# One stage with one weight ring for merge, output projection and feed-forward, and the second norm's token factor moved behind the products

## The chip, the cores and the metric

The kernel runs on one core of one Trainium2 chip. The metric is the device time of one execution in microseconds (us); a kernel is given as the median of several executions.

## The reference, cut to what matters

One decoder layer for 1,024 prompt tokens and 8 sample tokens, 1,032 in all. The attention and the recurrence ahead of this part are not touched. Their outputs `o_nsa` and `o_hg` enter here:

```python
ga, gb = jnp.split(mg, 2, axis=-1)              # mg: columns of xn @ w_in
y_a = o_nsa @ w_nsa_out
y_b = o_hg @ w_hg_out
x = x + (sigmoid(ga) * y_a + sigmoid(gb) * y_b) @ w_o
xn2 = rms_norm(x, norm2_g)                      # x * rsqrt(mean(x^2) + eps) * g
ext = concatenate([conv_state, xn2 @ w_gate])
c = conv_b + sum(conv_w[j] * ext[:, j:j + L] for j in range(3))
x = x + (silu(c) * (xn2 @ w_up)) @ w_down
```

Outputs of this part are `y`, the last gate rows (`conv_*`) and the window rows (`win_*`), the latter mostly a copy of the old ones. D_MODEL is 1024, D_FF is 2816.

## The kernel before, in words

Channels lie on the 128 partitions and the 1,032 tokens along the free axis, as 8 channel tiles (KD) and three token pieces of 344 (TC).
Every large product is made in three passes (`three_pass`, L305): weights and activations are split into a high part (a rounded copy, ScalarE) and a low part (the rest, a VectorE subtraction), and TensorE accumulates high x high, high x low, low x high. A weight unit is 128 output columns over all 8 channel tiles (512 KB): SyncE loads it into `raw`, ScalarE writes `wh`, VectorE writes `wl` and frees `raw`; two units are in flight. One unit is 3 x 8 x 3 = 72 matmuls of 344 columns.

The last part of the program is this row of blocks:

- `merge_gates` (L321) loops 4 times over two channel tiles. One unit is a pair of gate columns (a and b, two DMAs); for each token piece TensorE makes 48 matmuls for the two gates and then 8 plain fp32 ones for the outputs of the two mixers (L438; each shows as two records). ScalarE takes the sigmoid (L378), VectorE multiplies twice (L409) and adds into `x2` (L413).
- `split_merged` (L444) makes high and low parts of the merged rows in `xh` and `xl`.
- `project_out` (L461) multiplies by `w_o` in 8 units; VectorE adds the product and the residual rows read back from DRAM (L514).
- `norm_to_split` (L242) squares `x2` (L260), adds up (L273), sums over channels with 3 plain fp32 matmuls (L300), takes reciprocal (L279) and root (L262), scales each row by gain and token factor (L290) and splits again (L265, L284).
- `conv_ffn` (L541) has three blocks. The first copies the old window rows DRAM to DRAM (L577, 4 MB) and loads the conv state behind it on the same queue (L580), which TensorE turns (L588) and VectorE copies (L595). The second is the feed-forward: hidden tiles in groups of 6, 6, 6 and 4 (`FF_GROUPS`), per tile a gate unit and an up unit; then 8 down units per group. ScalarE takes the gate product out of PSUM (L633), VectorE does the convolution (L681 to L693), ScalarE Silu (L641), VectorE multiplies with the up product (L698). The third turns the gate tail (L765), copies it (L771) and stores it.
- `store_y` (L784) turns `x2` back (L802), copies it over three buffers and stores it (L830).

Of the kernel before, what the change touches and what calls it, by code (L numbers as in the profile page):

```python
# [10 lines left out]
F32 = mybir.dt.float32  # L11
# [230 lines left out]
def norm_to_split(c, gain, tag):  # L242

    nc = c.nc
    low0 = c.base
    sq = c.low("sq" + tag, [P, 2, NT])
    acc = c.low("acc" + tag, [P, NT])
    rs = c.low("rs" + tag, [P, NT])
    tmp = c.low("ntmp" + tag, [P, 2, NT])
    sqd, added, ssum = c.sem("sqd" + tag), c.sem("added" + tag), c.sem("ssum" + tag)  # L250
    inv, rsq, scaled, hi_done, lo_done = (c.sem(x + tag) for x in ("inv", "rsq", "scaled", "hi", "lo"))
    with nc.Block() as block:

        @block.scalar
        def _(act):
            act.activation(acc[:, :], c.x2[:, 0, :], ACT.Square).then_inc(sqd, 1)
            for k in range(1, KD):
                if k >= 3:
                    act.wait_ge(added, k - 2)
                act.activation(sq[:, k % 2, :], c.x2[:, k, :], ACT.Square).then_inc(sqd, 1)  # L260
            act.wait_ge(inv, 4)
            act.activation(rs[:, :], acc[:, :], ACT.Sqrt).then_inc(rsq, 1)  # L262
            for k in range(KD):
                act.wait_ge(scaled, k + 1)
                act.activation(c.xh[:, k, :], tmp[:, k % 2, :], ACT.Copy).then_inc(hi_done, 1)  # L265

        @block.vector
        def _(dve):
            for k in range(1, KD):
                dve.wait_ge(sqd, k + 1)  # L270
                if k > 1:
                    dve.wait_ge(added, k - 1)
                dve.tensor_tensor(acc[:, :], acc[:, :], sq[:, k % 2, :], ALU.add).then_inc(added, 1)  # L273
            dve.wait_ge(ssum, 1)
            for t in range(3):
                dve.tensor_scalar(rs[:, t * TC:(t + 1) * TC], c.psum[:, t, 0:TC], 1.0 / D, EPS,
                                  ALU.mult, ALU.add).then_inc(inv, 1)
            dve.wait_ge(inv, 3)
            dve.reciprocal(acc[:, :], rs[:, :]).then_inc(inv, 1)  # L279
            dve.wait_ge(rsq, 1)  # L280

            def low_part(k):
                dve.wait_ge(hi_done, k + 1)
                dve.tensor_tensor(c.xl[:, k, :], tmp[:, k % 2, :], c.xh[:, k, :].bitcast(F32),  # L284
                                  ALU.subtract).then_inc(lo_done, 1)

            for k in range(KD):
                if k >= 2:
                    dve.wait_ge(lo_done, k - 1)
                dve.scalar_tensor_tensor(out=tmp[:, k % 2, :], in0=c.x2[:, k, :], scalar=c.ct[:, gain + k:gain + k + 1],  # L290
                                         in1=rs[:, :], op0=ALU.mult, op1=ALU.mult).then_inc(scaled, 1)
                if k >= 1:
                    low_part(k - 1)
            low_part(KD - 1)

        @block.tensor
        def _(pe):
            pe.wait_ge(added, KD - 1)
            for t in range(3):
                mm = pe.matmul(c.psum[:, t, 0:TC], c.ones[:, :], acc[:, t * TC:(t + 1) * TC], start=True, stop=True)  # L300
            mm.then_inc(ssum, 1)
    c.base = low0

def three_pass(pe, out, parts, first=True, last=True):  # L305

# [8 lines left out]
def wait_turn(c, sp, sem, value):  # L315

    sp.wait_ge(sem, value)
    sp.sem_inc(c.turns, 1)

def merge_gates(c, io):  # L321

    nc = c.nc
    low0 = c.base
# [2353 lines left out]
```

## Time and profile before

| | |
|---|---|
| median of 3 runs | 2265.21 us (2257.08 to 2267.87) |
| the profiled execution | 2267.54 us, its span 2265.6 us |
| TensorE busy | 2015.7 us, 89% of the span |
| VectorE, ScalarE busy | 812.5 us (36%), 592.6 us (26%) |
| mean granted TensorE clock | 0.931 of full |
| first matmul of the merge to the last of the feed-forward | 1000.8 to 2237.6 us |

The page gives busy time per engine, the span in 40 slices, and the costliest groups. The windows view cuts the span into stretches and gives for each what every engine did and the clock TensorE was granted (1.00 is 2.4 GHz, 0.50 is 1.2 GHz). The timeline gives single instructions with the idle time ahead of them and what ended it.

### The profile page before, as it was taken

How to read it: one execution, taken by the hardware profiler on the slowest of the kernel's cores; microseconds unless marked ns; L12 is line 12 of the kernel's file. 1: busy time of each engine (PE TensorE's matmuls, PEld its weight loads, DVE VectorE, ACT ScalarE, POOL GpSimd, SP SyncE). 2: the span in 40 equal slices, each digit the busy share in tenths (PEclk: the TensorE clock that was granted, in tenths of full speed). 3: DMA queues.
4: the chain of work that ended last, by engine and by line, in shares of the span. 5: the costliest groups of instructions: out<-in, count | busy, mean ns of one | idle time of the engine just before them, and what ended most of it. 6: DMA issues, size and time to landing. Idle time of an engine off the chain costs nothing. (4 is left out here: it accounts for less than half of the span.)

```text
span 2265.6 us, 40273 instructions
## 1 busy us (share of the span) xinstructions
PE 2015.7 (89%) x16434; PEld 1763.6 (78%) x16434; DVE 812.5 (36%) x1614; ACT 592.6 (26%) x1174; POOL 155.1 (7%) x214
## 2 busy tenths in 40 slices
PE   4999899999776899879999878079999999999997
PEld 3767755655554898768888778079999999999996
DVE  5223045555312466511211122523323333332333
ACT  5133156555202143310110111222212211221221
POOL 3000001000210223300000000000000000000000
PEclk8899869999897999879999989589999999999999
DMA  8324251000335312131211031121111111111112
GB/s 233 55 69 165 106 136 52 1 1 1 103 121 193 105 32 58 40 75 29 56 33 32 0 102 47 66 67 46 44 58 37 44 49 47 46 40 53 47 37 88
DMA packets 164458, 148.04 MB, mean 65 GB/s; under 512 B 7561, under 2 KB 151898, under 8 KB 163466
## 3 DMA queue, kind: packets, MB, share of 16 engines
q1 hardware_dynamic: 153260, 123.77, 18.0%
q0 software_dynamic: 6208, 17.67, 3.1%
q10 hardware_dynamic: 4864, 4.84, 0.9%
q8 instruction: 89, 1.46, 0.3%
q14 instruction: 37, 0.30, 0.1%
HBM read 120.54 MB, written 29.99 MB: 66 GB/s over the span
## 5 line engine op out<-in xcount | busy, mean ns | idle before, releaser
L309 PE MATMUL psum<-xh,fwh 128*128 128x344 f32 x1056 | 339.0, 321 | 7.6 <-DVE fwl L668 7.6
L310 PE MATMUL psum<-xl,fwh 128*128 128x344 f32 x1056 | 338.4, 320 | 0.0
L311 PE MATMUL psum<-xh,fwl 128*128 128x344 f32 x1056 | 338.3, 320 | 0.0
L309 PEld LDWEIGHTS psum<-xh,fwh 128*128 128x128 f32 x1056 | 199.1, 189 | 7.7 <-issue 7.7
L311 PEld LDWEIGHTS psum<-xh,fwl 128*128 128x128 f32 x1056 | 199.2, 189 | 0.0
L310 PEld LDWEIGHTS psum<-xl,fwh 128*128 128x128 f32 x1056 | 199.0, 188 | 0.0
L311 PE MATMUL psum<-hh,fwl 128*128 128x344 f32 x528 | 169.2, 320 | 0.0
L309 PE MATMUL psum<-hh,fwh 128*128 128x344 f32 x528 | 169.2, 320 | 0.0
L310 PE MATMUL psum<-hl,fwh 128*128 128x344 f32 x528 | 169.1, 320 | 0.0
L309 PE MATMUL psum<-xh,mwh 128*128 128x344 f32 x384 | 130.2, 339 | 15.6 <-DVE mwl L394 15.6
L623 ACT ACTIVATE fwh<-fraw 128x1024 fp32r<-128x1024 f32 x76 | 80.3, 1056 | 200.9 <-PE psum L311 197.2
L309 PE MATMUL psum<-wh_n,xh 128*128 128x512 f32 (+3 forms) x288 | 113.3, 393 | 20.5 <-DVE wl_n L913 20.5
L310 PE MATMUL psum<-xl,mwh 128*128 128x344 f32 x384 | 123.6, 322 | 0.0
L311 PE MATMUL psum<-xh,mwl 128*128 128x344 f32 x384 | 123.5, 322 | 0.0
L309 PE MATMUL psum<-xh,r_wh 128*128 128x344 f32 x288 | 103.5, 360 | 7.8 <-DVE r_wl L1578 7.8
L310 PE MATMUL psum<-wl_n,xh 128*128 128x512 f32 (+3 forms) x288 | 109.2, 379 | 0.0
L311 PE MATMUL psum<-wh_n,xl 128*128 128x512 f32 (+3 forms) x288 | 108.9, 378 | 0.0
L409 DVE TENSOR_TENSOR msg<-msg,psum 128x344 f32<-128x344 f32 x48 | 22.4, 509 | 238.4 <-ACT msg L378 238.4
L309 PEld LDWEIGHTS psum<-hh,fwh 128*128 128x128 f32 x528 | 99.3, 188 | 0.0
L311 PEld LDWEIGHTS psum<-hh,fwl 128*128 128x128 f32 x528 | 99.3, 188 | 0.0
L310 PEld LDWEIGHTS psum<-hl,fwh 128*128 128x128 f32 x528 | 99.2, 188 | 0.0
L713 DVE TENSOR_TENSOR x2b<-x2b,psum 128x1032 f32 (+1 forms) x32 | 39.3, 1230 | 165.0 <-PE psum L311 165.0
(422 smaller groups left out, 3746.1 us busy)
## 6 DMA issues: line engine op xcount, KB each, us to landing
fraw<-in_w_gate SPq DMA_DIRECT2D x22, 512.0 KB, 3.8
fraw<-in_w_up SPq DMA_DIRECT2D x22, 512.0 KB, 3.9
fraw<-in_w_down SPq DMA_DIRECT2D x24, 384.0 KB, 3.1
cmp_pages<-in_cache_kv SPq DMA_DIRECT2D x64, 128.0 KB, 2.1
mraw<-in_w_in SPq DMA_DIRECT2D x16, 512.0 KB, 5.5
raw_n<-in_w_in SPq DMA_DIRECT2D x24, 256.0 KB, 3.5
r_raw<-in_w_in SPq DMA_DIRECT2D x12, 512.0 KB, 3.9
xh_copy<-xh SPq DMA_DIRECT2D x1, 4128.0 KB, 12.7
```

Of the source, the lines that this page charges most:

```text
L309: pe.matmul(out, wh, xh, start=(first and k == 0), stop=False)
L310: pe.matmul(out, wh, xl, start=False, stop=False)
L311: mm = pe.matmul(out, wl, xh, start=False, stop=(last and k == n - 1))
L409: dve.tensor_tensor(sg[:, n % 2, g, :], sg[:, n % 2, g, :], c.psum[:, 4 * (n % 2) + 2 + g, 0:TC], ALU.mult).then_inc(prod if g == 0 else b ...
L623: act.activation(wh[:, b, :, :], raw[:, b, :, :], ACT.Copy).then_inc(hi, 1)
L713: dve.tensor_tensor(y, y, c.psum[:, 3 * b:3 * b + 3, 0:TC], ALU.add).then_inc(bank_free[b], 1)
```

## The change

All blocks from `merge_gates` to the feed-forward become one block, `finish`; `store_y` takes over the gate tail.

- **One ring.** The two `raw`/`wh`/`wl` buffers serve 16 gate units (gates a and b are units of their own now), 8 units of `w_o` and all feed-forward units in one sequence. Merge and output projection are written out straight instead of in loops, and so is the first hidden tile.
- **Merge.** Per unit and token piece: 24 gate matmuls, 4 plain ones, in one of four pairs of PSUM banks. The merged rows are split as they are made, into `mh` and `ml`.
- **First unit of the projection and first gate unit** run channel tile by channel tile (`by_channel`), each tile waiting for its low part alone.
- **Norm.** `gh` and `gl` are parts of `x2 * gain` without the token factor, made as each `x2` row is done. The factor `rs` is computed beside the first gate and up units, and is multiplied into the gate product as VectorE takes it out of PSUM (ScalarE did that before) and into the Silu output. That is two multiplications of 1,032 columns per hidden tile.
- **DMAs.** The conv state is loaded and turned ahead of the first gate unit. The window copy is made as 8 DMAs, behind the loads of units 4 to 11. The gate tail is turned after `y` in `store_y`.

Core of the diff: the call, then pieces of SyncE's part, of VectorE's (the projection, then the hidden tile) and of TensorE's. ScalarE's part is not shown; it makes `mh`, `gh`, the squares and `wh` in the same order.

```diff
-    merge_gates(c, io)
-    split_merged(c)
-    project_out(c, io)
-    norm_to_split(c, 8, "2")
-    conv_ffn(c, io)
-    store_y(c, io)
+    finish(c, io, xh_at, onsa_at)
...
+            for u in range(NM):
...
+                if u >= 2:
+                    sp.wait_ge(raw_free, u + 1)
+                sp.dma_start(raw[:, g, :, :], w_v[:, :, at:at + P]).then_inc(w_in[g], 16)
+                if u == 0:
+                    sp.dma_start(state_rows[:, :], rows16).then_inc(st_in, 16)
+                if u >= 2:
+                    sp.wait_ge(pair, 3 * (u - 2) + 3)
...
+                if 4 <= u < 12:
+                    s = u - 4
+                    sp.dma_start(io["win_sample"][0, s, 0:511].rearrange("t a g d -> (t a g d)"),
+                                 io["state_kv_win"][0, s, 1:512].rearrange("t a g d -> (t a g d)")).then_inc(win, 16)
...
+            for w in range(NO):
+                b = w % 2
+                low(U0 + w + 1, 1 - b)
+                dve.wait_ge(prod[b], w // 2 + 2)
+                dve.wait_ge(r_in[b], 16 * (w // 2 + 1))
+                dve.tensor_tensor(three(x2[:, w, :]), c.psum[:, 3 * b:3 * b + 3, 0:TC], three(res[:, b, :]), ALU.add).then_inc(bank_free[b], 1)
+                if w:
...
+                    dve.tensor_tensor(acc[:, :], acc[:, :], sq[:, :], ALU.add).then_inc(summed, 1)
+                dve.wait_ge(g_hi, w + 1)
+                dve.scalar_tensor_tensor(out=gl[:, w, :], in0=x2[:, w, :], scalar=c.ct[:, 8 + w:9 + w],
+                                         in1=gh[:, w, :].bitcast(F32), op0=ALU.mult, op1=ALU.subtract).then_inc(g_lo, 1)
...
+            def tile(g, i, first):
+                low(i * 2 + (units[g] + 1), 1)
+                if first:
+                    scale()
+                    low(units[g] + 2, 0)
+                    dve.memset(gate[:, 0:2], 0.0)
+                    dve.wait_ge(root, 1)
+                dve.wait_ge(prod[0], i + (h0 + (2 - BASE)))
...
+                dve.tensor_tensor(three(gate[:, 2:2 + NT]), c.psum[:, 0:3, 0:TC], three(rs[:, :]), ALU.mult).then_inc(bank_free[0], 1)
...
+                dve.tensor_tensor(act_c[:, :], act_c[:, :], rs[:, :], ALU.mult).then_inc(act_scaled, 1)
...
+            def by_channel(b, xh, xl, ready, each, between=None):
+                for k in range(KD):
+                    if k == KD - 1 and between:
+                        between()
+                    pe.wait_ge(ready, each * (k + 1))
...
+            for w in range(NO):
...
+                if w < 2:
+                    pe.wait_ge(m_free, 3 * NM - (2 if w == 0 else 1))
+                if w == 0:
+                    by_channel(0, mh, ml, m_lo, 3)
+                else:
+                    by_token(b, mh, ml)
+            def sums():
+                pe.wait_ge(summed, KD - 1)
+                for t in range(3):
+                    if t == 2:
+                        pe.wait_ge(ms, 1)
+                    pe.matmul(c.psum[:, 6 + t % 2, 0:TC], c.ones[:, :], acc[:, cols(t)], start=True, stop=True).then_inc(ssum, 1)
```

How the order of instructions moves, at three places. **TensorE at the end of the merge, before**: the last plain products of the merge (`mwy`), a loop's end, two block ends, and the first matmuls with `w_o` (`owh`, `owl`).

```order
L438 MATMUL psum<-o_nsa,mwy 128x344 x4
L438 MATMUL psum<-o_hg,mwy 128x344 x4
L424 REGISTER_ALU
L424 COMPARE_AND_BRANCH
L338 UNCONDITIONAL_BRANCH
L523 UNCONDITIONAL_BRANCH
L526 UNCONDITIONAL_BRANCH
L526 ISA
L529 REGISTER_ALU
L309 MATMUL psum<-xh,owh 128x344
```

**The same place now** (`t_wh`, `t_wl` are the ring's parts, `mh`, `ml` those of the merged rows):

```order
L247 MATMUL psum<-xl,t_wh 128x344
L248 MATMUL psum<-xh,t_wl 128x344
L637 MATMUL psum<-o_hg,t_wy 128x344 x4
L246 MATMUL psum<-mh,t_wh 128x344
L247 MATMUL psum<-ml,t_wh 128x344
L248 MATMUL psum<-mh,t_wl 128x344
```

Nothing stands between the two products any more, neither a branch nor a block end.

**VectorE from the last row of the projection into the first hidden tile, now** (L488 is a low part of weights, L523 the residual sum, L536 and L538 the token factor):

```order
L523 TENSOR_TENSOR x2b<-psum,t_res 128x1032
L528 TENSOR_TENSOR t_acc<-t_acc,t_sq 128x1032
L530 SCALAR_TENSOR_TENSOR xgl<-x2b,ct,xgh 128x1032
L488 TENSOR_TENSOR t_wl<-t_raw,t_wh 128x1024
L536 TENSOR_SCALAR rs_14609<-psum 128x344 x3
L538 RECIPROCAL t_acc<-rs_14609 128x1032
L488 TENSOR_TENSOR t_wl<-t_raw,t_wh 128x1024
L547 MEMSET gate 128x2
L553 TENSOR_TENSOR gate<-psum,rs_14609 128x1032
L560 TENSOR_SCALAR act_c<-gate,ct 128x1024
```

The 7 additions, 8 scalings and 8 splits that stood in a row of their own are gone from here; the reciprocal stands ahead of the low part for the second gate unit.

**SyncE's queue in the merge, now** (before, the window copy was one DMA of shape 8x8x16352, with `state_rows` right behind it):

```order
L342 DMA t_raw<-in_w_in 128x8x128
L349 DMA t_wy<-in_w_nsa_out 64x4x128 x2
L354 DMA out_win_sample<-in_state_kv_win 16x8176
L342 DMA t_raw<-in_w_in 128x8x128
L351 DMA t_wy<-in_w_hg_out 128x4x128
L354 DMA out_win_sample<-in_state_kv_win 16x8176
```

Each eighth of the copy now stands ahead of the load of the next unit.

## Rows read from the trace of the kernel before

**Rows 1.** The page, busy time, share of the span and instructions

```profile
PE 2015.7 (89%) x16434; PEld 1763.6 (78%) x16434; DVE 812.5 (36%) x1614; ACT 592.6 (26%) x1174; POOL 155.1 (7%) x214
```

**Rows 2.** The windows view, from the recurrence's last matmul to the end

```profile
core 0: us, PE busy (x) PEld busy (x) DVE busy (x) ACT busy (x) POOL busy (x), PEclk, DMA share, GB/s
985.24:1000.83 15.59, 0.01 (x1) 0.01 (x1) 3.31 (x5) 6.82 (x8) 1.09 (x2) 0.61 0.65 154
1000.83:1295.39 294.56, 294.55 (x1536) 256.23 (x1536) 49.43 (x83) 31.91 (x60) 0.00 (x0) 0.99 0.13 35
1295.39:1314.83 19.44, 0.00 (x1) 0.01 (x1) 11.92 (x12) 9.60 (x11) 0.00 (x0) 0.60 0.27 85
1314.83:1407.98 93.15, 93.15 (x576) 92.87 (x576) 16.65 (x14) 7.44 (x7) 0.00 (x0) 0.97 0.25 73
1407.98:1487.61 79.63, 6.35 (x30) 4.28 (x29) 39.13 (x31) 22.15 (x21) 0.00 (x0) 0.52 0.18 68
1487.61:2237.60 749.99, 749.70 (x4752) 749.42 (x4752) 261.69 (x283) 149.61 (x163) 0.00 (x0) 1.00 0.15 45
2237.60:2265.60 28.00, 12.37 (x94) 11.04 (x94) 10.27 (x11) 5.36 (x9) 0.00 (x0) 0.81 0.42 159
```

**Rows 3.** Timeline of the second boundary: start, length, instruction, idle time before it

```profile
1420.91 3.81 PE L300 MATMUL psum<-acc,ones 128*128 128x344 f32 x6 [12.93 <-DVE acc L273]
1426.16 6.60 DVE L279 RECIPROCAL acc<-rs 128x1032 f32<-128x1032 f32 x1
...
1477.50 2.53 PE L588 MATMUL psum<-ident,state_rows 16*128 16x16 f32 x22 [52.77 <-DMA state_rows<-in_state_conv]
```

**Rows 4.** Timeline: first matmul at each stretch's start or at full pace

```profile
1314.83 0.65 PE L309 MATMUL psum<-xh,owh 128*128 128x344 f32 x1 [19.44 <-DVE owl L504]
...
1319.84 0.32 PE L311 MATMUL psum<-xh,owl 128*128 128x344 f32 x1
...
1490.56 0.32 PE L310 MATMUL psum<-xl,fwh 128*128 128x344 f32 x1
```

**Rows 5.** The first DMA of the merge, and issues by line, KB each, us to landing

```profile
990.80 1.03 SPq L351 DMA_DIRECT2D mraw<-in_w_in  x2
...
fraw<-in_w_gate SPq DMA_DIRECT2D x22, 512.0 KB, 3.8
out_win_sample<-in_state_kv_win SPq DMA_DIRECT2D x1, 4088.0 KB
state_rows<-in_state_conv SPq DMA_DIRECT2D x1, 176.0 KB, 22.7
```

**Rows 6.** Groups by line on VectorE and ScalarE: count, busy us, mean ns

```profile
L409 DVE TENSOR_TENSOR msg<-msg,psum 128x344 f32<-128x344 f32 x48 | 22.4, 509 | 238.4 <-ACT msg L378 238.4
L394 DVE TENSOR_TENSOR mwl<-mraw,mwh 128x1024 fp32r<-128x1024 f32 x15 | 17.7, 1219 | 4.0 <-ACT mwh L365 4.0
L290 DVE SCALAR_TENSOR_TENSOR ntmp<-x2b,ct,rs 128x1032 f32<-128x1032 f32 x8 | 10.3, 1293 | 1.3 <-ACT rs L262 1.1
L514 DVE TENSOR_TENSOR x2b<-psum,ores 128x1032 f32 (+1 forms) x8 | 9.9, 1233 | 74.6 <-PE psum L311 74.6
L378 ACT ACTIVATE msg<-psum 128x344 f32<-128x344 f32 x48 | 19.3, 455 | 260.0 <-PE psum L438 260.0
L260 ACT ACTIVATE sq<-x2b 128x1032 f32<-128x1032 f32 x7 | 7.3, 1059 | 1.4 <-DVE acc L273 1.4
L262 ACT ACT_TABLE_LOAD x1 | 1.3, 1283 | 0.0
```

**Rows 7.** Timeline behind the feed-forward

```profile
2238.90 2.56 PE L765 MATMUL psum<-ident,gate_tail 128*10 128x128 f32 x22 [1.59 <-PEq L597]
2241.50 3.08 DVE L771 COPY rows_out<-psum 10x2816 f32<-10x2816 f32 x1 [2.92 <-PE psum L765]
...
2248.36 8.77 PE L802 MATMUL psum<-ident,x2b 128*128 128x128 f32 x64 [6.89 <-PEq L760]
...
2263.09 0.30 SPq L830 DMA_DIRECT2D out_y_sample<-ys  x1
```

More of the change, by code:

```diff
@@ L239, in load_and_norm @@
     c.base = low0
[L242 to L302, printed above, removed]
@@ L538 @@
[L538 to L563 removed]
+    hg_v = io["w_hg_out"][0].rearrange("(k p) n -> p k n", p=P)
@@ L568, in conv_ffn @@
     starts = [sum(FF_GROUPS[:g]) for g in range(len(FF_GROUPS))]
-    units = [2 * starts[g] + KD * g for g in range(len(FF_GROUPS))]
+    units = [F0 + 2 * starts[g] + KD * g for g in range(len(FF_GROUPS))]
     GEND = len(FF_GROUPS) - 1
+    BASE = NM // 2
+    cols = lambda t: slice(t * TC, (t + 1) * TC)
+    three = lambda x: x.rearrange("p (u t) -> p u t", u=3)
     with nc.Block() as block:
@@ L601, in load @@
+            residual(NO - 1)
             def load(u, b, src, at, nk):
@@ new lines, in tile @@
+                if not first:
+                    high_in_loop(i * 2 + (units[g] + 2), 0, i + (h0 + 1))
+                act.wait_ge(cv, i * 6 + (6 * t0 + 12))
+                act.activation(act_c[:, :], act_c[:, :], ACT.Silu).then_inc(act_done, 1)
+                act.wait_ge(hid_done, i + (t0 + 1))
+                act.activation(hh[:, bass.ds(i, 1), :].rearrange("p a t -> p (a t)"), hid[:, :], ACT.Copy).then_inc(hh_done, 1)
+            for g, n in enumerate(FF_GROUPS):
+                if g == 0:
+                    tile(0, 0, True)
+                with act.Fori(1 if g == 0 else 0, n) as i:
+                    tile(g, i, False)
+                h1 = units[g] // 2 + n
@@ L705, in _ @@
+                if g == 0:
+                    tile(0, 0, True)
+                with dve.Fori(1 if g == 0 else 0, n) as i:
+                    tile(g, i, False)
                 h1 = units[g] // 2 + n
@@ new lines, in sums, with product @@
+            def sums():
+                pe.wait_ge(summed, KD - 1)
+                for t in range(3):
+                    if t == 2:
+                        pe.wait_ge(ms, 1)
+                    pe.matmul(c.psum[:, 6 + t % 2, 0:TC], c.ones[:, :], acc[:, cols(t)], start=True, stop=True).then_inc(ssum, 1)
+            def product(u, b, half, first=False):
+                pe.wait_ge(raw_free, u + 3)
+                pe.wait_ge(bank_free[b], half + (1 - BASE))
+                if first:
+                    by_channel(b, gh, gl, g_lo, 1, sums)
+                else:
+                    by_token(b, gh, gl)
@@ L803, in _ @@
                     mm.then_inc(yt, 1)
+            pe.wait_ge(ev_a, 8)
+            pe.wait_ge(ev_v, 8)
+            for k in range(KF):
+                mm = pe.transpose(c.psum[0:10, 2 + k // 4, (k % 4) * P:(k % 4 + 1) * P], tail[:, k, :], c.ident[:, :])
+            mm.then_inc(tail_t, 1)
         @block.scalar
```

554 lines of the change are left out of this document (239 added, 315 removed).

## The prediction, made before the changed kernel ran

> **What bounds the kernel now.** The page first: TensorE is busy for 89% of the span, VectorE and ScalarE for 36% and 26% [rows 1]. So time can only come from TensorE's work or from the places where it stands still. The windows view shows these places: in the merge, the projection and the feed-forward TensorE is busy without a break (294.55 of 294.56, 93.15 of 93.15 and 749.70 of 749.99 us), and between them it does almost nothing for 15.59, 19.44, 79.63 and, at the end, some 16 of 28.00 us [rows 2]. The 79.63 are, by the timeline, a wait for the last sum of squares (12.93), the sums (3.81), 52.77 us until the conv state has landed, its turning (2.53) and 7.6 for the first weights [rows 3]. The reader is to see two things: no stretch of matmuls can be shortened by making another engine faster, and each boundary between stretches is paid in full. Each also leaves TensorE at its low level: the granted clock is 0.60 and 0.52 in the two gaps [rows 2], and the matmuls behind the first run at half pace for 5.01 us, 1314.83 to 1319.84 [rows 4], 17 starts where a full-pace start is 0.157 apart (749.99 us / 4752 = 0.158 agrees [rows 2]).
>
> **The change part by part.** TensorE's matmuls stay the same in number: 1152 and 192 plain ones (two records each), 576, 3 sums, 4752.
>
> *Boundary of merge and projection.* Removed: 19.44 us of standing still [rows 2] and the slow starts, 5.01 - 17 x 0.157 = 2.3 us [rows 4]. What has to hold: `w_o`'s first unit is loaded and split during the last gate unit, which needs VectorE and ScalarE for 1.2 and 1.1 us of its 18; and the last merged row comes in time. TensorE has channel tiles 0 to 6 to do first, 63 starts x 0.157 = 9.9 us. The chain in that time is sigmoid 0.46, product 0.51, sum 0.5, high part 0.5, low part 0.5 [rows 6]: 2.5 us, about 4 with the two other pieces in front. Covered with 6 us to spare, so 0 is added. Second unit of `w_o`: one table load of 1.28 stands ahead of its high part; ready some 6.5 us after the merge ends, wanted after 11.3.
>
> *Boundary of projection and feed-forward.* Removed: 79.63 us [rows 2] and the slow starts behind it, ten up to 1490.56 [rows 4]: 2.95 - 10 x 0.157 = 1.4 us. Added on TensorE: the three sums. They took 3.81 at half clock [rows 3], so 1.9 at the full one, with up to 0.3 of waiting for VectorE to free a bank. Together +2.2. Per row of the projection VectorE now does residual sum 1.23, square sum 1.23, low part 1.29 and a weight part 1.22, 5.0 us; ScalarE 3 x 1.06 [rows 6]; a unit lasts 11.3. After the last row at time t: sum of squares until t+3.9, `gl` until t+5.2, while TensorE has 9.9 us of gate unit without channel tile 7. No wait.
>
> *First hidden tile.* The tight place. Sums done at t+11.9; VectorE scales (1.5 us) and takes 6.60 for the reciprocal [rows 3], to t+20; the low part of the second gate unit to t+21.2, root and Silu table on ScalarE beside it (1.06 + 1.28 [rows 6], t+22.4), gate product times `rs` 1.23: bank free at t+22.4 (it waits for the root alone, not for the table). TensorE ends the first up unit at t + 11.3 + 2.2 + 11.3 = t+24.8 and wants the bank then. 2.4 us to spare. The tile after it: convolution some 4.5 us (three steps as in L290's row, a little less, and three short ones), Silu 1.1, times `rs` 1.2, times up 1.2: t+30.5, low part of the next up weights by t+34.5, wanted at t+36.1. I add 0.
>
> *Feed-forward in its steady state.* VectorE gets two operations of 1.23 us per hidden tile, of the kind of L514 [rows 6], ScalarE loses one. VectorE had 261.69 us in 749.99 [rows 2]; 22 x 2.46 = 54 more make 316, 42%. The gate bank comes free after 1.23 instead of ScalarE's copy of about the same, 11 us before it is wanted, and the multiplication by `rs` ends before the up product does. Added: 0. If that cover failed, each of 22 tiles would pay its lateness.
>
> *Start.* From the first DMA to the first matmul it is 10.03 us now (990.80 [rows 5] to 1000.83 [rows 2]). Then: one load instead of two (3.8 to landing [rows 5]), the conv state behind it (176 KB, a third of 512, +1.3), turning 2.53 [rows 3], its copy 0.5, low part 1.22: 9.35. I take -0.7; bounds are -2.0 (state lands with the weights) and +1.0 (the 6.3 us in which the two loads landed together now also holds for these two).
>
> *Window copy.* 4 MB took the queue about 21 us, by the 22.7 that the conv state behind it needed [rows 5]. Now eight parts of 2.7 us, each ahead of one weight load (3.8) that has 18 us of TensorE work to hide in. 0; both ends of its cost are in the rivals.
>
> *End.* The gate tail's block is gone from ahead of `store_y`: its matmuls start at 2238.90 instead of 2248.36 [rows 7], -9.5. Added behind it: turning, mostly beside the last copies of `y`, one copy of 3.08 and two DMA issues, about 3.9 to 4.9 after the point where the last DMA of `y` is issued now [rows 7]. I take +4.7: -4.8.
>
> **Sum**, against the profiled execution: 2267.5 - 19.4 - 2.3 - 79.6 - 1.4 + 2.2 - 0.7 - 4.8 = **2161.5 us**. The profiled execution lies 2.3 above the median of 2265.2, so the median by this is 2159.2; I give **2160**. A measurement of this kernel can tell about 0.5% (11 us) from no change.
>
> **A rule weighed against the trace.** The merge loop turned 4 times before, the projection loop 4 times, and nothing in the rows shows a cost of a turn: 294.55 of 294.56 us busy, 93.15 of 93.15 [rows 2]. At most 0.01 us can be gained by writing them out. The Trainium skill says in "Runtime: NRT & Kernel Launch", section "Instruction fetch mechanics", that a taken branch out of the fetched window stalls the engine until its target is fetched. By that rule each turn of such a body should have cost something, and the straight program would gain more than my sum. Priced by TensorE's nearest row at a block's entry (1.59 us [rows 7]) that estimate is 8 x 1.6 = 13 us more, 2147. The rows stand against it; it gets a chance of 0.02.
>
> **The rivals.**
>
> *A boundary still holds TensorE.* The chain at the first hidden tile is 20 us long on paper with 2.4 to spare, and the three others have 6 to 10. If semaphore hops or a late reciprocal eat that, TensorE waits a few us, at worst once more at half clock. For it: the reciprocal is one piece of 6.60 us between other work. Against: no VectorE group in these rows runs longer than its mean. Price 3 to 20 us (the whole first boundary would be 19.4): 2163 to 2180.
>
> *The window copy gets into the weight ring's way.* If each eighth ran as slowly as the whole did, 21 us instead of 2.7, it would outlast the 18 us unit beside it, and the loads behind it would come late: 8 x 3 to 4 us, and a slow restart each, 2188 to 2200. Against: the order shows 16x8176 where 8x8x16352 stood, so the pieces are spread no worse than the whole was. The Trainium skill ("DMA: Bandwidth & Descriptors", "Why a DMA increments its semaphore by 16 and not by 1") has the number of DMA engines follow the slowest dimension, at most 16; by that rule this copy gets 16 instead of 8. No row here shows it.
>
> *Slower: the straight program cannot be fetched fast enough.* Merge, projection and first tile are now some 2,000 matmuls and as many weight loads in one line. If fetching them held each start back, the gain would be gone at 106 / 2000 = 0.053 us per matmul, that is starts 0.21 instead of 0.157 apart; at 0.08 the kernel takes 2320. Against: one turn of the merge loop is 384 matmul records of the same kind and runs without a break, as do the 749.70 us of the feed-forward at 0.158 a start [rows 2].
>
> *The change does not do what it says*, because waits that I read as met (three banks of the merge, the ring's turn) are met late everywhere: then the boundaries shrink, but merge units pay. Same prices as the first rival, counted there.
>
> **How the numbers follow.** The sum holds: 0.80, its own range 2151 to 2170 (start -1.3/+1.7, end +-1, the sums +-0.5, and the spread of 11 us that the runs before show around their median). Boundary rival: 0.10. Window copy: 0.04. Slower: 0.03. Branch rule: 0.02. The rest, 0.01, is no change. The range **2150 to 2177** takes the first case and most of the second and leaves out some 12%. Faster by over 0.5%: 0.96; within 0.5%: 0.01; slower: 0.03.
>
> **What would show it.** In the profile after: TensorE busy without a break from the first gate unit to the end of the feed-forward, about 1135 us; granted clock 1.00 there after the first 5 us; idle before the first matmul on `mh` and on `xgh` under 0.3 us; a busy time of VectorE near 860 us (812 + 54, less 8 splits of 1.2, more in the split of the merged rows, now in pieces); reciprocal beside matmuls; the three sums in about 2 us. A wait of TensorE for VectorE at the second gate unit shows the first rival, waits of ScalarE for `t_raw` between units 5 and 13 the second, starts more than 0.17 apart the third. I am wrong if the stretch of matmuls is longer than 1145 us.

## The result and the profile after

| | before | after |
|---|---|---|
| median of 4 runs each, side by side | 2261.14 us (2255.65 to 2267.87) | 2157.39 us (2153.18 to 2159.89) |
| ratio, 95% interval | | 0.9538 (0.9503 to 0.9572) |
| span of the profiled execution | 2265.6 us | 2151.5 us |
| first matmul of the merge to last of the feed-forward | 1236.2 us | 1133.5 us |
| VectorE, ScalarE busy | 812.5, 592.6 us | 860.3, 573.1 us |
| mean granted TensorE clock | 0.931 | 0.955 |

The forecast was 2160 us with 2150 to 2177 as its range. Later runs of the same two kernels side by side gave 2156.36 (6 runs) against 2261.77 us (8 runs), ratio 0.9536 (0.9518 to 0.9555).

Top of the page of the kernel after, its answer to [rows 1]:

```profile
span 2151.5 us, 39896 instructions
PE 2005.3 (93%) x16434; PEld 1754.7 (82%) x16434; DVE 860.3 (40%) x1666; ACT 573.1 (27%) x1168; POOL 155.2 (7%) x214
PEclk8899959999979699977999999999999999999999
```

TensorE is busy for 10 us less than before, in a span that is 114 us shorter. From slice 20 on (1022 us) PEclk stands at 9 throughout.

The windows view after, with the stretches of [rows 2] (start, merge, projection, feed-forward with the three sums behind its first seven channel tiles, end). Columns: stretch, length, busy time and records of each engine, granted clock, DMA share, GB/s:

```profile
980.23:996.21 15.98, 2.52 (x22) 2.42 (x22) 2.66 (x6) 6.94 (x8) 1.09 (x2) 0.61 0.56 110
996.21:1290.11 293.90, 293.90 (x1536) 255.81 (x1537) 63.76 (x107) 43.73 (x83) 0.00 (x0) 0.99 0.19 56
1290.11:1380.98 90.87, 90.87 (x578) 90.77 (x577) 36.03 (x33) 25.51 (x27) 0.00 (x0) 1.00 0.35 99
1380.98:2130.00 749.02, 748.99 (x4760) 747.73 (x4758) 327.24 (x334) 132.01 (x145) 0.00 (x0) 1.00 0.15 44
2130.00:2151.50 21.50, 10.62 (x95) 9.51 (x94) 10.52 (x11) 5.37 (x9) 0.00 (x0) 0.91 0.54 203
```

The two rows of 19.44 and 79.63 us in [rows 2] have no answer here: each stretch starts where the one before ends. Matmuls run without a break for 1133.5 us. Stretch by stretch, against [rows 2] (there the last matmul of the feed-forward ends at 2237.31, 0.3 us ahead of the window's bound):

| stretch | before | after | change | forecast |
|---|---|---|---|---|
| what both kernels do alike, up to the start | 985.24 | 980.23 | -5.0 | 0 |
| start | 15.59 | 15.98 | +0.4 | -0.7 |
| merge | 294.56 | 293.90 | -0.7 | 0 |
| boundary merge / projection | 19.44 | 0 | -19.4 | -19.4 |
| projection | 93.15 | 90.87 | -2.3 | -2.3 |
| boundary projection / feed-forward | 79.63 | 0 | -79.6 | -79.6 |
| feed-forward with sums | 749.70 | 749.02 | -0.7 | +0.8 |
| end | 28.29 | 21.50 | -6.8 | -4.8 |

The 5.0 us in front are no work of the change: in eleven other profiles the last matmul before the start ended between 970.0 and 986.6 us, for versions of either kernel, so the front scatters. Without it the change took 109.1 us off the span; the forecast's terms make 106.0.

The start, in the timeline after (start, duration, engine, line, operation; in brackets the idle time ahead and what ended it):

```profile
985.41 0.39 SPq L342 DMA_DIRECT2D t_raw<-in_w_in  x1
985.84 0.57 SPq L344 DMA_DIRECT2D state_rows<-in_state_conv  x1
990.64 1.06 ACT L401 ACTIVATE t_wh<-t_raw 128x1024 fp32r<-128x1024 f32 x1 [3.95 <-DMA t_raw<-in_w_in]
991.94 2.52 PE L616 MATMUL psum<-ident,state_rows 16*128 16x16 f32 x22 [11.71 <-DMA state_rows<-in_state_conv]
994.50 0.53 DVE L484 COPY conv_state<-psum 128x352 f32<-128x352 f32 x1 [10.13 <-PE psum L616]
996.21 0.66 PE L246 MATMUL psum<-xh,t_wh 128*128 128x344 f32 x1 [1.75 <-DVE t_wl L488]
```

The weights' high part is done at 991.70; its low part (1.2 us) would let the first gate matmul go at 992.9. It goes at 996.21, since VectorE stands first in line for the turned conv state, which landed 6.1 us after its issue and whose turning took 2.52. Experiment 10 takes this wait away.

The first hidden tile, in the timeline after:

```profile
1390.85 2.19 PE L673 MATMUL psum<-t_acc,ones 128*128 128x344 f32 x6
1392.62 0.58 PE L246 MATMUL psum<-xgh,t_wh 128*128 128x344 f32 x1
1393.63 6.60 DVE L538 RECIPROCAL t_acc<-rs 128x1032 f32<-128x1032 f32 x1
1400.27 1.07 ACT L445 ACTIVATE rs<-t_acc 128x1032 f32<-128x1032 f32 x1 [4.65 <-DVE t_acc L538]
1401.37 1.23 DVE L553 TENSOR_TENSOR gate<-psum,rs 128x1032 f32<-128x1032 f32 x1
1405.64 0.32 PE L246 MATMUL psum<-xgh,t_wh 128*128 128x344 f32 x1
```

The reciprocal of [rows 3] is still there with the same 6.60 us, now beside gate matmuls. The gate product ends at 1402.60 and frees the bank. With t = 1380.8, the end of the projection, that is t+21.8 (forecast t+22.4), and TensorE opens the next gate unit at 1405.64, t+24.8 as forecast: 3.0 us to spare where 2.4 had been worked out.

The end, in the timeline after:

```profile
2131.59 8.05 PE L729 MATMUL psum<-ident,x2b 128*128 128x128 f32 x72 [1.59 <-PEq L332]
2142.21 2.56 PE L734 MATMUL psum<-ident,gate_tail 128*10 128x128 f32 x22 [2.56 <-DVE ys L753]
2143.43 0.32 SPq L764 DMA_DIRECT2D out_y_sample<-ys  x1
2144.81 3.08 DVE L755 COPY rows_out<-psum 10x2816 f32<-10x2816 f32 x1 [1.45 <-PE psum L734]
2148.20 0.28 SPq L767 DMA_DIRECT2D out_conv_sample<-rows_out  x1
```

Against [rows 7]: `y` is turned right behind the feed-forward (9.5 us sooner behind it, as forecast), its last store is issued 11.84 us after that instead of 14.73, and from there to the end of the span it is 8.07 instead of 2.51 us.

### The profile page after: what moved, and what is told of

Same layout as the page of the kernel before. It is cut to its first block and busy times, and to the rows that moved or that the text cites. A ratio compares the mean times of both kernels' runs of the same rounds, so it can differ in the third digit from the quotient of the medians.

```text
span 2151.5 us, 39896 instructions
## 1 busy us (share of the span) xinstructions
PE 2005.3 (93%) x16434; PEld 1754.7 (82%) x16434; DVE 860.3 (40%) x1666; ACT 573.1 (27%) x1168; POOL 155.2 (7%) x214
## 5 line engine op out<-in xcount | busy, mean ns | idle before, releaser
L246 PE MATMUL psum<-xgh,t_wh 128*128 128x344 f32 x1056 | 338.0, 320 | 0.0
L247 PE MATMUL psum<-xgl,t_wh 128*128 128x344 f32 x1056 | 337.3, 319 | 0.0
L248 PE MATMUL psum<-xgh,t_wl 128*128 128x344 f32 x1056 | 337.2, 319 | 0.0
L248 PEld LDWEIGHTS psum<-xgh,t_wl 128*128 128x128 f32 x1056 | 198.5, 188 | 0.0
L247 PEld LDWEIGHTS psum<-xgl,t_wh 128*128 128x128 f32 x1056 | 198.3, 188 | 0.1
L246 PEld LDWEIGHTS psum<-xgh,t_wh 128*128 128x128 f32 x1056 | 198.3, 188 | 0.1
L246 PE MATMUL psum<-hh,t_wh 128*128 128x344 f32 x528 | 168.7, 319 | 0.0
L247 PE MATMUL psum<-hl,t_wh 128*128 128x344 f32 x528 | 168.3, 319 | 0.0
L248 PE MATMUL psum<-hh,t_wl 128*128 128x344 f32 x528 | 168.0, 318 | 0.0
L246 PE MATMUL psum<-xh,t_wh 128*128 128x344 f32 x384 | 136.3, 355 | 1.7 <-DVE t_wl L488 1.7
L488 DVE TENSOR_TENSOR t_wl<-t_raw,t_wh 128x1024 fp32r<-128x1024 f32 x100 | 121.9, 1219 | 34.3 <-ACT t_wh L436 29.2
L246 PE MATMUL psum<-wh_n,xh 128*128 128x512 f32 (+3 forms) x288 | 113.0, 392 | 19.5 <-DVE wl_n L850 19.4
```

The lines of the kernel that those rows point to most:

```text
L246: pe.matmul(out, wh, xh, start=(first and k == 0), stop=False)
L247: pe.matmul(out, wh, xl, start=False, stop=False)
L248: mm = pe.matmul(out, wl, xh, start=False, stop=(last and k == n - 1))
L488: dve.tensor_tensor(wl[:, b, :, :], raw[:, b, :, :], wh[:, b, :, :].bitcast(F32), ALU.subtract).then_inc(raw_free, 1)
```

## The experiments

Each run below is one execution beside one of the kernel before unless said otherwise. Totals scatter with the front by several us, so the verdicts go by "the stretch", first matmul of the merge to the start of the last feed-forward matmul: 1133.5 us in the changed kernel's profile and 1134.1 in a second one; 1236.2 in the kernel before.

**1. The window copy earlier, in the kernel before.** The DMA moves from ahead of the conv state's load to behind the merge's last weight load.

```diff
@@ merge_gates, SyncE, behind its loads @@
+            sp.dma_start(io["win_sample"][0, :, 0:511]..., io["state_kv_win"][0, :, 1:512]...).then_inc(win, 16)
@@ conv_ffn, SyncE @@
-            sp.dma_start(io["win_sample"][0, :, 0:511]..., io["state_kv_win"][0, :, 1:512]...).then_inc(win, 16)
```

> The kernel before, with the window copy issued behind the last weight load of the merge instead of ahead of the conv state's load. My theory: of the 79.63 us between projection and feed-forward only the state's wait behind the 4 MB copy goes, 22.7 us to landing become 4 to 6 (6.1 was measured in the changed kernel), so that stretch is 61 to 63 us and the kernel about 17 to 19 us faster. The merge and the projection stay as they are, because the copy takes 21 us in the shade of 18 us units. Rival, that the copy disturbs the weight loads wherever it lies: the merge or the projection gets longer by 5 to 20 us and nothing is won. Rival, that the state's load is slow by itself: no change.

Measured: 2245.36 against 2267.79 us. The second boundary in the windows view, and its wait in the view of TensorE's waits (us in total, times, longest). Below them, from the timeline of the kernel before, the last low part of the norm and the issue of the state's load:

```profile
1404.24:1463.99 59.75, 6.65 (x31) 4.30 (x30) 39.13 (x31) 22.16 (x21) 0.00 (x0) 0.54 0.08 21
```

```profile
PE psum L589 <- DMA state_rows<-in_state_conv: 32.5, 1, 32.5
```

```profile
1452.36 1.23 DVE L284 TENSOR_TENSOR xl<-ntmp,xh 128x1032 fp32r<-128x1032 f32 x1
...
1454.76 0.43 SPq L580 DMA_DIRECT2D state_rows<-in_state_conv  x1
```

The wait for the conv state shrinks from 52.8 [rows 3] to 32.5 us, the boundary from 79.6 to 59.75, which is 1.3 us below the range expected, and the stretch to 1217.6 (-18.6). Merge and projection stay as they were. So of the 79.6 us some 20 were the window copy in the queue: the state's load took 3.3 us here and 22.7 behind the copy. The rest was there without it, and most of it is the norm. The 52.77 us of [rows 3] bear the name of the state's load, but that load was issued only at 1454.76, behind the norm's block; for the first 30 of them TensorE stood still for VectorE's and ScalarE's work on the norm (VectorE is busy for 39 us of the boundary in both kernels).

**2. The ring cold at the first boundary.** The first unit of `w_o` is loaded and split only when the last row is merged; all else is the changed kernel. SyncE's and VectorE's part; ScalarE's high part moves in the same way.

```diff
             for w in range(NO):
                 u = U0 + w
+                if w == 0:
+                    sp.wait_ge(merged, 3 * KD)
...
-                low(u + 1, 1 - g)
+                if u < NM - 1:
+                    low(u + 1, 1 - g)
...
             merged_low(KD - 1)
+            low(U0, 0)
```

> The changed kernel with the load of the first output-projection unit held back until the last merged row is there, as a block's end would; the rows are still split as they are made. My theory: TensorE waits for 1.9 us of merging, 4 to 5 us of load, 1.1 for the high and 1.2 for the low part, 8 to 9.5 us, and restarts at half clock for 1 to 2 us: 10 to 11 us slower than the changed kernel, the rest of the old 19.44 us being the split of the rows. Rival, that the load is short against the chain of the last row anyway: 5 us or less.

Measured: 2165.01 us, stretch 1144.25 (+10.8). Windows behind the merge, then TensorE's waits:

```profile
1289.61:1298.22 8.61, 0.45 (x2) 0.00 (x1) 3.54 (x6) 4.04 (x7) 0.00 (x0) 0.73 0.59 183
1298.22:1305.00 6.78, 6.78 (x27) 6.78 (x28) 1.23 (x1) 1.05 (x1) 0.00 (x0) 0.59 0.75 233
```

```profile
PE psum L246 <- DVE t_wl L492: 8.2, 1, 8.2
```

The gap is 8.4 us longer than a normal step, and the 6.78 us behind it ran at a mean granted clock of 0.59, which makes the projection 93.25 instead of 90.87: +2.4. That is the kernel before in small: 19.44 us and 2.3 of slow starts [rows 2, 4].

**3. No channel-by-channel units.** First unit of the projection and first gate unit wait for all eight low parts.

```diff
                 if w == 0:
-                    by_channel(0, mh, ml, m_lo, 3)
-                else:
-                    by_token(b, mh, ml)
+                    pe.wait_ge(m_lo, 3 * KD)
+                by_token(b, mh, ml)
...
                 if first:
-                    by_channel(b, gh, gl, g_lo, 1, sums)
+                    pe.wait_ge(g_lo, KD)
+                    by_token(b, gh, gl)
+                    sums()
```

> The changed kernel with both channel-by-channel units made token piece by token piece again, so that each needs the last channel tile at once. My theory: TensorE waits 3.2 us for the last merged low part at the first boundary and 5.2 us for the last row of the norm at the second, 8.5 us together, and the clock stays at its full level or loses at most 2 us. Rival, that the ring alone carries the gain and these last rows are in time anyway: under 2 us. Rival, that each stop of a few us costs a restart at half clock as the long ones did: 12 us or more.

Measured: 2173.11 us, stretch 1146.1 (+12.7). TensorE's waits, then windows behind the first gap (two), of the second gap and behind it:

```profile
PE psum L246 <- DVE xgl L530: 5.0, 1, 5.0
PE psum L246 <- DVE ml L494: 3.0, 1, 3.0
```

```profile
1299.40:1303.28 3.88, 3.88 (x16) 3.88 (x17) 1.23 (x1) 1.46 (x2) 0.00 (x0) 0.59 0.74 216
1303.28:1307.28 4.00, 4.00 (x26) 4.00 (x26) 0.00 (x0) 0.00 (x0) 0.00 (x0) 0.97 1.02 314
...
1391.54:1396.84 5.30, 0.32 (x3) 0.06 (x2) 3.81 (x4) 3.06 (x3) 0.00 (x0) 0.89 0.00 0
1396.84:1400.20 3.36, 3.36 (x12) 3.36 (x13) 0.99 (x1) 0.00 (x0) 0.00 (x0) 0.50 0.25 72
```

The waits are 8.0 us, about what was expected. The total is 4.7 us more. Behind each gap the starts lie 0.29 us apart instead of 0.157, 11 of them behind the first (1.5 us) and 19 behind the second (2.5 us). The rival, that each short stop costs a slow restart too, holds; the theory of 8.5 us with at most 2 us of slow starts falls.

**4. The token factor before the products.** The sums go first, and TensorE waits for the root before the first gate unit, as if the factor still had to be in the operand. It isn't multiplied in there; only the wait is made. On ScalarE, not shown, the high part of the second gate unit moves behind the root.

```diff
                 if first:
-                    by_channel(b, gh, gl, g_lo, 1, sums)
+                    sums()
+                    pe.wait_ge(root, 1)
+                    by_channel(b, gh, gl, g_lo, 1)
```

> The changed kernel, in which TensorE makes the three sums and waits for the finished token factor before the first gate unit; all else, the split of rows without the factor too, stays. My theory: the time is that of the chain sum of squares (3.9 us after the last row's product), sums 1.8, scaling 0.6, reciprocal 6.6, root 1.1, so TensorE stands 14 to 15 us at this place and then restarts at half clock for 1 to 2 us: 15 to 17 us slower than the changed kernel. Rival, that the chain is hidden by nothing even now (it only moved to the second gate unit): the changed kernel would wait there as well and this one costs under 5 us more.

Measured: 2175.23 us, stretch 1150.7 (+17.2). TensorE's waits in the stretch, and the window from the projection's last matmul to the first gate matmul:

```profile
PE psum L246 <- ACT rs L444: 8.3, 1, 8.3
PE psum L673 <- DVE t_acc L528: 3.8, 1, 3.8
PE psum L673 <- DVE rs L536: 1.3, 1, 1.3
```

```profile
1385.64:1402.27 16.63, 3.23 (x10) 1.22 (x8) 12.77 (x8) 4.16 (x5) 0.00 (x0) 0.67 0.11 33
```

13.4 us are waiting, the rest are sums and first gate matmuls at the low clock. So the two operations that the change adds to every hidden tile buy this: with weights and rows prepared as here, waiting for the factor alone leaves 17 us at the boundary. Rows that really had to be multiplied by it and split behind that wait would add to this; that was not run.

**5. Two more VectorE operations per hidden tile.** They take the maximum of the Silu output with itself, so nothing changes in the output.

```diff
                 dve.tensor_tensor(act_c[:, :], act_c[:, :], rs[:, :], ALU.mult).then_inc(act_scaled, 1)
                 dve.wait_ge(act_scaled, i + (t0 + 1))
+                dve.tensor_tensor(act_c[:, :], act_c[:, :], act_c[:, :], ALU.max).then_inc(twice, 1)
+                dve.wait_ge(twice, i * 2 + (2 * t0 + 1))
+                dve.tensor_tensor(act_c[:, :], act_c[:, :], act_c[:, :], ALU.max).then_inc(twice, 1)
+                dve.wait_ge(twice, i * 2 + (2 * t0 + 2))
```

> The changed kernel with VectorE's added work in the hidden tiles doubled: two more operations of 1,032 columns on the Silu output (a maximum of it with itself, which changes nothing), 22 x 2 x 1.23 = 54 us more on VectorE, in the chain that ends in the hidden tile. Theory: VectorE idles 1.3 us per tile ahead of the product with the up projection, so the hidden tile comes 1.2 us later, which is hidden in every group of 6 (the down unit has 5 other tiles, 7.1 us, to do first) and shows by under 1 us in the group of 4: the feed-forward is 748.7 to 750 us long. Rival, that the two multiplications by the token factor already eat into TensorE: each tile pays 1.2 us or more, 26 us in all.

Measured: 2158.61 us; feed-forward from first to last start 749.97 against 748.70 us, stretch 1134.8. Window of the feed-forward and VectorE's timeline in the last hidden tile:

```profile
1383.40:2133.50 750.10, 749.02 (x4759) 747.79 (x4759) 381.52 (x378) 131.98 (x145) 0.00 (x0) 1.00 0.15 44
```

```profile
2088.80 1.23 DVE L583 TENSOR_TENSOR hid<-act_c,psum 128x1032 f32<-128x1032 f32 x1
2091.38 1.23 DVE L587 TENSOR_TENSOR hl<-hid,hh 128x1032 f32 x1 [1.35 <-ACT hh L456]
```

54 us more of VectorE (381.5 against 327.3) cost 1.3 us, all of it one stop in the last hidden tile, where the low part of the hidden rows comes at 2092.6 and the down unit had gone ahead to 2091.5. In the other 21 tiles two more operations are free as well. VectorE is half idle there, yet what bounds an addition is this one chain; the change's own two operations left it some 1.2 us (2.5 added, a stop of 1.37 between two starts that otherwise lie 0.157 us apart).

**6, 7. How much the first hidden tile has to spare.** One, then four more passes over the mean square, in place, ahead of the reciprocal. They too leave the output as it is.

```diff
                 dve.wait_ge(ms, 3)
+                for j in range(4):
+                    dve.tensor_tensor(rs[:, :], rs[:, :], rs[:, :], ALU.max).then_inc(longer, 1)
+                    dve.wait_ge(longer, j + 1)
                 dve.reciprocal(acc[:, :], rs[:, :]).then_inc(inv, 1)
```

> The changed kernel with one more VectorE pass over the 1,032 columns (1.23 us, to start of the next 1.26) between the mean square and the reciprocal; the output does not change. The chain of the first hidden tile gets 1.26 us longer. In the changed kernel the gate product of that tile ended 2.6 us before TensorE wanted the bank. Theory (the slack is what the trace shows): the product ends about 1402.6 + 1.3 on the old scale, 1.3 us in time, TensorE has no gap, the stretch of matmuls stays at 1133.5 us. Rival (TensorE wants something else of that chain earlier than I read, such as the low part behind the reciprocal): a gap of up to 1.3 us and a stretch of 1134.5 or more.

> The changed kernel with four such passes, 5.0 us. By the slack of 2.6 us TensorE now stops for 2.4 us before the second gate unit. Two theories of what a short stop costs: (a) only its own length, since a stop of 2.4 us is shorter than the two (3.3 and 5.3 us between starts) behind which the granted clock read 0.5: stretch 1133.5 + 2.4 = 1135.9 and granted clock 1.00 behind it. (b) as behind those two, a stretch of 0.5 clock of some 3 to 7 us, 1.7 to 3.4 us more: stretch 1137.6 to 1139.3. Rival to both: the slack is not there, and the gap is 3.5 us or more.

Measured: with one, 2158.16 us, no gap, stretch 1133.5. With four, 2159.89 us, stretch 1135.8. TensorE's waits, and windows up to the gap, in it and behind it, with four:

```profile
PE psum L246 <- DVE gate L557: 1.9, 1, 1.9
```

```profile
1393.80:1408.42 14.62, 14.59 (x88) 13.64 (x87) 13.26 (x9) 1.20 (x2) 0.00 (x0) 1.00 0.01 2
1408.42:1410.67 2.25, 0.33 (x4) 0.04 (x2) 2.17 (x4) 2.22 (x3) 0.00 (x0) 1.00 0.02 5
1410.67:1414.67 4.00, 4.00 (x25) 4.00 (x26) 3.65 (x6) 0.51 (x2) 0.00 (x0) 1.00 0.44 128
```

The slack is as the trace of the changed kernel shows it, 3.0 us: one more pass leaves 1.8 of it, and with four, 5.0 us added, TensorE stops for 2.1 us beyond its pace, a gap of 2.24 between two starts. And this stop costs only itself. Behind it the granted clock stays at 1.00, 2.4 GHz, where it had gone to 1.2 GHz behind the gaps of 3.47 and 5.30 us in experiment 3. Theory (a) holds for this place (and the gap of 1.37 us in experiment 5 left the clock at 1.00 too). What else than the gap's length differs between the three places was not separated.

**8. The loops of the kernel before written out.** `pe.Fori` of merge and projection becomes a Python loop.

```diff
-            with pe.Fori(0, KD // 2) as i:
+            for i in range(KD // 2):
```

> The kernel before, with TensorE's part of the merge and of the output projection written out straight instead of in loops of four turns; the other engines keep their loops. My theory: no cost of a turn was in the rows, so the merge stays 314.0 us from its first matmul to the projection's first and the projection's 576 matmuls take 92.8, both within 0.5 us. The rival from the Trainium skill ("Runtime: NRT & Kernel Launch", "Instruction fetch mechanics"), by which a taken branch stalls the fetch: up to 1.6 us less per turn, 13 us in all. The rival that straight code is fetched too slowly: starts more than 0.158 us apart and both stretches longer.

Measured: 2250.65 against 2251.8 us. Windows of merge and projection:

```profile
985.00:1278.50 293.50, 293.37 (x1536) 255.27 (x1536) 49.43 (x84) 31.92 (x60) 0.00 (x0) 0.99 0.13 36
...
1298.60:1391.00 92.40, 92.40 (x576) 92.29 (x576) 16.65 (x14) 7.43 (x7) 0.00 (x0) 0.98 0.25 74
```

From first to last start the merge is 0.8 us and the projection 0.5 us shorter than in the kernel before; the stretch is not (1236.4 against 1236.2). The difference lies in the starts at the low clock, 0.29 us apart, that open each part: 11 instead of 17 in the merge, 13 instead of 17 in the projection, but 19 instead of 10 in the feed-forward, which the edit does not touch. At 0.13 us each they make the 0.8, the 0.5 and the 1.1 us by which the feed-forward is longer. Their number scatters from run to run: the merge of one and the same kernel, the changed one, took 293.9 us with 15 of them and 294.5 with 20. What is left for the turns of the loops can't be told from zero, and the straight program costs nothing either.

**9. The window copy as one DMA** behind the load of unit 4, in the changed kernel.

```diff
-                if 4 <= u < 12:
-                    s = u - 4
-                    sp.dma_start(io["win_sample"][0, s, 0:511]..., io["state_kv_win"][0, s, 1:512]...).then_inc(win, 16)
+                if u == 4:
+                    sp.dma_start(io["win_sample"][0, :, 0:511]..., io["state_kv_win"][0, :, 1:512]...).then_inc(win, 16)
```

> The changed kernel with the window copy as one DMA of 4 MB behind the fourth gate unit's loads, in the shape it had before, instead of eight. Theory now: the load of a unit is issued while the unit two ahead of it runs, so it has 18 us until ScalarE wants it and 36 until TensorE does; a copy of 21 us ahead of it makes it land some 7 us after ScalarE would take it and still 10 us ahead of TensorE. Merge 293.9 us as it is, nothing lost. My rival of the prediction had one unit of cover only: 6 us and more of standing still in the merge, with a restart at half clock.

Measured: 2159.7 us, stretch 1133.4, merge 293.9, no gap. From issue to landing of six loads of weights around it, in the tile view, first of this kernel, then of the changed one, where five of the six stand behind an eighth of the copy:

```profile
DMA to landing us min/median/max: 3.9/5.1/24.3
```

```profile
DMA to landing us min/median/max: 5.0/5.3/5.9
```

And ScalarE's timeline at the high part that this load feeds:

```profile
1086.59 1.06 ACT L400 ACTIVATE t_wh<-t_raw 128x1024 fp32r<-128x1024 f32 x1 [8.05 <-DMA t_raw<-in_w_in]
```

The load behind the copy needs 24.3 us, its high part comes 8 us late, and TensorE doesn't notice: the load was issued at 1062.3, its low part is done at 1088.9, and the unit that uses it begins at 1095.9. Cutting the copy in eight bought nothing; moving it did (experiment 1).

**10. Both ends, 5 runs beside others of the changed kernel and the kernel before.** The conv state is loaded with the second unit and turned behind the first one, and the gate tail is turned and copied in six pieces between the tiles of `y`.

```diff
-                if u == 0:
+                if u == 1:
                     sp.dma_start(state_rows[:, :], rows16).then_inc(st_in, 16)
...
-            pe.wait_ge(st_in, 16)
-            for k in range(KF):
...
+                if u == 1:
+                    pe.wait_ge(st_in, 16)
+                    for k in range(KF):
...
+                r = tt - 1
+                if 0 <= r < 6:
...
+                    for k in range(4 * r, min(4 * r + 4, KF)):
```

> The changed kernel with its two ends mended: the conv state is turned behind the first gate unit instead of ahead of it, and the gate tail is turned and copied in six pieces between the tiles of y, split over ScalarE and VectorE, so that its two DMAs leave ahead of the last tile of y. Theory: the first matmul of the merge comes 2.5 to 3.5 us earlier (16.2 us after the recurrence become 13), TensorE pays 1.5 to 2.5 us for the turning inside the merge, and the stretch behind the feed-forward becomes 4.5 to 5.5 us shorter, 21.8 to 17: 5 to 7 us less in all, about 0.3%. Rival, that the pieces delay the tiles of y, whose stores set the pace there: the end gains under 2 us and the whole is the same.

> The changed kernel again, as the measure for the next one on the same chip. From the first matmul of the merge to the last of the feed-forward 1133 to 1134 us, as in its first profile; the stretch ahead of it, which the change does not touch, has moved by up to 6 us between profiles and will do so again; 2150 to 2162 us in all.

Measured: 2152.27 us (5 runs, 2142.93 to 2153.40), 0.9503 of the kernel before (0.9479 to 0.9527); the changed kernel in the same session 2156.36 (2144.08 to 2158.02), 0.9536. Windows of the start, of the merge and of the end:

```profile
985.96:997.92 11.96, 0.32 (x4) 0.04 (x2) 2.18 (x4) 5.88 (x7) 1.09 (x2) 0.66 0.52 123
997.92:1293.96 296.04, 296.04 (x1558) 257.64 (x1559) 64.36 (x108) 44.75 (x84) 0.00 (x0) 0.99 0.20 57
...
2134.10:2151.70 17.60, 10.45 (x94) 9.56 (x94) 8.72 (x13) 6.78 (x12) 0.00 (x0) 0.96 0.66 248
```

The first window begins with the recurrence's last matmul, 0.3 us before its end. From that end the start is 11.6 us, 4.3 shorter than in the changed kernel, 1.5 to 2.1 of which come back as the turning inside the merge, and the end is 3.7 us shorter (17.9 against 21.5). From the end of the unchanged front to the end of the span the profiles give 1165.5 us against 1171.3 and 1172.0 for the changed kernel. So the whole came as expected, 6 us, but not its parts: the start gained more than the 2.5 to 3.5 us expected, the end less than the 4.5 to 5.5. The two kernels' total times still overlap, so in total this is the fastest version measured, by some 4 us of median that one measurement does not secure.

## Why the prediction was right

*Both boundaries.* The terms that carried the sum, 19.4 + 2.3 and 79.6 + 1.4 us, came out whole: the stretches meet. Experiments 2 to 4 show what keeps them shut, each by taking one thing away: the warm ring (10.8 us), the order by channel tile (12.7), the factor on the products (17.2). Experiment 1 shows some 20 us of the second boundary to be the window copy. The rest of the 102.7 us, the norm's row of scalings and splits above all, is read from the timelines and was not taken back alone; nor was a block's end tried apart from the cold ring and the unsplit rows behind it. The cover of 9.9 us at the first boundary, 6 of them to spare, is borne out by experiment 3: without it TensorE waits 3.0 us for the last low part. At the second boundary it waits 5.0, where `gl` had been put at t+5.2.

*The wait of 52.77 us* was read as time until the conv state had landed. Experiment 1 shows that some 30 us of it were the norm. The sum did not hang on this, since the change takes both away.

*First hidden tile, "the tight place".* 2.4 us to spare were worked out, 3.0 are in the trace, and experiments 6 and 7 confirm them from both sides. The rival that a boundary still holds TensorE was therefore a real one, but a small overrun would have cost less than its price of 3 to 20 us: a stop of 2.1 us there made the feed-forward 2.2 us longer.

*Feed-forward.* 0 for two VectorE operations is right, with VectorE at 327.2 us where 316 was given (the norm's reciprocal and what stands around it are the other 11). The forecast did not see that the last tile is the narrowest: there 1.2 us were left.

*Sums.* +2.2 us was forecast; the next gate matmul starts 1.8 us after the first of them, at a granted clock of 1.00. With the slow starts gone the row was to be 0.8 us longer, and it is 0.7 shorter. The sums account for 0.4 of the 1.5 us; the rest is a pace of 0.1572 us a start where the kernel before had 0.1574, and why is open.

*The start has the wrong sign:* -0.7 was taken, +0.4 came, within the bounds given (-2.0 to +1.0). The step that failed is the conv state's landing. It was priced at 3.8 + 1.3 = 5.1 us behind the first load's issue; its turning began 6.5 us behind it (985.41 to 991.94). That is 1.4 us of the 1.45 by which the first matmul came late on the prediction's own measure: 10.80 us behind the first DMA (985.41 to 996.21), where 9.35 had been worked out. The stretch is only 0.4 longer because that DMA is issued 0.4 us sooner behind the recurrence.

*The end is mis-sized:* -4.8 forecast, -6.8 measured. Its first half (-9.5) is exact. The second, +4.7, came as +2.7: -2.9 in front of the last store of `y`, which no step foresaw, and +5.6 behind it, where 3.9 to 4.9 stood. In the kernel before `y` was turned behind a stop of 6.89 us [rows 7], with a granted clock of 0.80; that fits the -2.9, but no run separates it. Part of the size is scatter: in the nine profiles with this end it was 21.5 us five times and 22.9 to 23.1 four times. In a longer one (experiment 5) the gate tail was turned in 4.18 us at a clock of 0.60, in the one above in 2.56 at 1.00:

```profile
2146.03 4.18 PE L739 MATMUL psum<-ident,gate_tail 128*10 128x128 f32 x22 [2.56 <-DVE ys L758]
```

*The rule on branches.* By the rows a turn of a loop cost nothing, and experiment 8 agrees: the stretch is 1236.4 us without the eight turns and 1236.2 with them. The Trainium skill ("Runtime: NRT & Kernel Launch", "Instruction fetch mechanics") says that a taken branch out of the fetched window stalls the engine. By that rule the eight turns, at the forecast's 1.6 us each, were worth 13 us; this trace does not show them.

*The window copy's rival* was priced wrongly: "the 18 us unit beside it" as cover, with 3 to 4 us lost per eighth. The cover is nearly two units, 34 us (1062.3 to 1095.9 in experiment 9). Even the whole copy in one piece costs nothing (experiment 9). The Trainium skill's rule on the number of DMA engines ("DMA: Bandwidth & Descriptors", "Why a DMA increments its semaphore by 16 and not by 1"), on which that rival was weighed, decided nothing here: how many engines each form of the copy got was not tried apart.

*The slower case*, a straight program that can't be fetched, is ruled out for this size: starts are 749.02 / 4760 = 0.157 us apart, and no gap above 0.6 us lies in the 1133.5 us.

*How far it was luck.* Outside the front the change took 3 us more than forecast: the end, the feed-forward and the merge gave 2.0, 1.5 and 0.7 us more, the start 1.1 us less. The 2160 and the median of 2157.4 are nearer each other than the terms secure, since the median moves by several us with a front that no term speaks of.

## What to carry to other kernels

When one engine is busy without a break inside its stages, count its time between them, and ask of each boundary three things: are the next weights split, can the next product start on the part of the rows that is ready, and can a factor that needs all the rows be multiplied in behind the product. Here taking away each of the three alone brought back 11 to 17 us. Then look for the narrowest chain by the time at which its result is wanted, not by an engine's share; VectorE, busy for 44% of the feed-forward, had 1.2 us to spare in one tile. And look when a load is issued before you put a wait down to it: of a wait of 52.8 us under a DMA's name 30 us were over before the load was issued.

## What the runs showed of the hardware

- A short stop can cost more than itself. Gaps of 3.47, 5.30 and 8.61 us between TensorE's starts were followed by stretches at 1.2 GHz, for 11, 19 and 19 starts 0.29 us apart, 1.4 to 2.7 us of loss each. Gaps of 1.37 and 2.24 us were not: granted clock 1.00 before, in and behind them.
- Because of that the price of a stall at a boundary here is its length plus some 2 us, as long as it is one of the longer ones, and two stalls can cost more than one of their summed length: 8.0 us of waits in two places became 12.7, one wait of 8.2 us became 10.8.
- A 4 MB copy from DRAM to DRAM held the load queued behind it for 24.3 us, against 5.0 to 5.9 for the six loads of that stretch where the copy goes in eighths.
- How many starts stay at the low clock when a stretch opens differs between runs of one kernel: 15 and 20 at the merge of the changed one, 0.6 us of difference.
